# Seven-product up projection of a fused decoder trunk: three products chained in one PSUM bank, the seventh one pair later

## The chip, the cores and the metric

One core of a Trainium2 chip. The metric is the device time of one execution of the whole program in microseconds.

## The reference

Two decoder layers over 1024 tokens of width 1024, all in float32. Layer 0 mixes with a gated DeltaNet, layer 1 with gated linear attention; after each mixer stands a feed-forward block, the part that the change touches:

```python
def conv_glu_ffn(h, w_up, conv_w, w_down):          # h (1, 1024, 1024), w_up (1024, 5632), w_down (2816, 1024)
    u = causal_depthwise_conv(h @ w_up, conv_w)     # 3 taps over the tokens, one set per channel
    gate, val = jnp.split(u, 2, axis=-1)
    return (jax.nn.silu(gate) * val) @ w_down
...
x = x + rms_norm(conv_glu_ffn(rms_norm(x, ffn_pre_norm[layer]), ...), ffn_post_norm[layer])
```

## The kernel before

**Matmuls.** Every float32 operand is kept as a high and a low part (fp32r). A product is three matmuls with 512 columns: high by high, high by low, low by high (`product3`, lines 80 to 82). All engines run their own hand-ordered list; semaphores hold them together.

**Up stage.** The 5632 output channels are 44 tiles of 128: 22 gate tiles and 22 value tiles, in pairs p = 0 to 21. Tokens are split in a near and a far half of 512, input channels in halves k1 and k2. Pairs 0 to 3 are done plainly. From pair 4 (`PLAIN`) on, a pair's 2 x 2 block product (two weight tiles, two token halves) is done with seven quarter products instead of eight (Winograd's form of Strassen). The names A11, A12, A22 are weight blocks, S1 to S4 sums of weight blocks, made by POOL in `sums` (line 404); t1, t2, t4 are sums of token blocks. One quarter product is 4 x 3 matmuls. PE's order in a pair (`seven_products`) is A11, S2, S3, S1, A22, A12, S4. The first three go to three quarters of two PSUM tensors `part_ps`, S1 and A22 to the far and near half of `gate_ps`, A12 and S4 to the near and far half of `value_ps`. A half is one bank.

**What follows a product.** ScalarE copies A11's product to SBUF (`keep_first`, line 489). VectorE joins the rest in seven additions (`products`, helper `join`, line 707), among them those into gate far, gate near, value near and value far. Then for the gate and the value tile each: ScalarE writes the last tap times the PSUM tensor (`scaled_gate` line 467, `scaled_value` line 476), VectorE adds the two other taps (`conv`, lines 693 and 698), ScalarE takes silu of the gate (line 481), and VectorE multiplies both (`activated`, line 704). The hidden tile goes to DRAM by SyncE.

**Weights.** Raw tiles arrive in a ring of four (`raw`). ScalarE makes the high part (`high`, `high_operand`, line 439), POOL the low part (`low`, line 398), into a ring of ten half slots that runs ahead of PE; a slot is free when `s_prod` shows its product done.

**Down stage.** 22 steps d for the near tokens, then 22 for the far. A step reads one hidden tile back: SyncE loads it into one of three buffers `h_raw` (`load_hidden`, line 339; from d = 3 on it waits until `hidden_low(d - 3)` has freed the buffer), ScalarE makes the high part (`high_hidden`, line 497), VectorE the low part (`hidden_low`, line 712). A step is 4 x 2 x 3 matmuls into the four PSUM tensors `down_ps`; `part_ps`, both, come first, then `gate_ps`, then `value_ps`. In step 0 PE waits before the third for the last gate convolution and before the fourth for the last value convolution (`s_conv`).

**The last pair.** In pair 21 the lists of both stages interleave. ScalarE: ..., `scaled_gate`, `high_hidden(2)`, a down weight, `silu`, `high_hidden(3)`, `scaled_value`, a down weight, `high_hidden(4)`. VectorE: `hidden_low(0)` and `hidden_low(1)` stand ahead of the join that waits for A22:

```python
            if p == FT - 1:
                hidden_low(0)
                hidden_low(1)
            dve.wait_ge(s_prod, task(p, A22) + 1)
            join(gate_ps[:, near], u3, gate_ps[:, near])
            conv(2 * p, gate_ps, gate, near_value)
            dve.wait_ge(s_prod, task(p, S4) + 1)
            join(value_ps[:, far], with_p5, value_ps[:, far])
            conv(2 * p + 1, value_ps, hid[p % 2])
```

Of the kernel before, what the change touches and what calls it, by code (L numbers as in the profile page):

```python
# [6 lines left out]
P = 128  # L7
# [69 lines left out]
def product3(pe, out, w_hi, w_lo, x_hi, x_lo, first, last):  # L77


    pe.matmul(out, w_hi, x_hi, start=first, stop=False)  # L80
    pe.matmul(out, w_hi, x_lo, start=False, stop=False)  # L81
    return pe.matmul(out, w_lo, x_hi, start=False, stop=last)  # L82
# [105 lines left out]
def feed_forward(nc, stack, layer, consts, w_up, conv_w, w_down, hidden, x_in, x_out, post_gain, pre_gain, x_hi, x_lo,  # L188
# [38 lines left out]
    p1, u2, u3, with_p5 = (kept[:, n, :] for n in range(4))  # L227

    gate_ps = ahead.banks
    value_ps = ps(n_ + "value", [P, T])  # L230
    part_ps = [ps(f"{n_}part{i}", [P, T]) for i in range(2)]
    down_ps = [*part_ps, gate_ps, value_ps]
# [8 lines left out]
    s_p1 = sem("first_product_kept")  # L241
    s_comb = sem("products_joined")
# [20 lines left out]
    A11, S2, S3, S1, A22, A12, S4 = range(7)  # L263
    FIRST_DOWN = 2 * PLAIN + 7 * (FT - PLAIN)
# [4 lines left out]
    def task(pair, operand):  # L269
        return 2 * PLAIN + 7 * (pair - PLAIN) + operand  # L270
# [36 lines left out]
    def operand_source(k):  # L307

        pair, operand = PLAIN + (k - 2 * PLAIN) // 7, (k - 2 * PLAIN) % 7
# [4 lines left out]
    def joined(pair, n):  # L314
        return 7 * (pair - PLAIN) + n
# [4 lines left out]
    def _(sp):  # L320
# [10 lines left out]
        def load_hidden(d):  # L331
# [3 lines left out]
            if d >= HIDDEN_RAWS:  # L335
                sp.wait_ge(s_hlo, d - HIDDEN_RAWS + 1)
            elif PLAIN < FT:
                sp.wait_ge(s_lo, FIRST_DOWN)
# [56 lines left out]
    def _(pool):  # L395
# [10 lines left out]
        def operands(pair):  # L406
            gates, values = raw[2 * pair % FFN_RAWS], raw[(2 * pair + 1) % FFN_RAWS]
            made = 4 * (pair - PLAIN)
            for n in (2 * pair, 2 * pair + 1):
# [3 lines left out]
            low(task(pair, A11), values[:, near])  # L413
            low(task(pair, S2), sums[:, 1, :])
            combine(2, values[:, near], gates[:, near], ALU.subtract, 0)
            low(task(pair, S3), sums[:, 2, :])
            low(task(pair, S1), sums[:, 0, :])
            low(task(pair, A22), gates[:, far])
            combine(3, values[:, far], sums[:, 1, :], ALU.subtract, made + 2)
            low(task(pair, A12), values[:, far])  # L420
            low(task(pair, S4), sums[:, 3, :])
# [3 lines left out]
        for pair in range(PLAIN, FT):  # L425
            operands(pair)
        for d in range(STEPS):
# [7 lines left out]
    def _(act):  # L435
# [17 lines left out]

        def token_sum_high(n, out):
# [5 lines left out]
        def scaled_gate(p):  # L460
            if p < PLAIN:
                act.wait_ge(s_prod, 2 * p + 1)
            else:
                act.wait_ge(s_comb, joined(p, 5))
# [4 lines left out]
        def scaled_value(p):  # L469
            if p < PLAIN:  # L470
                act.wait_ge(s_prod, 2 * p + 2)
            else:
                act.wait_ge(s_comb, joined(p, 7))
            if p >= 2:
                act.wait_ge(s_store[p % 2], 16 * (p // 2))
            act.activation(hid[p % 2][:, :], value_ps[:, :], ACT.Copy, scale=taps[:, FT + p, 2:3]) \
# [63 lines left out]
        for p in range(PLAIN):  # L540
            if p < PLAIN - 1:
                high(2 * p + 2)
            else:
                for operand in (A11, S2, S3):
                    high_operand(PLAIN, operand)
# [11 lines left out]
            else:  # L557
# [3 lines left out]
                for operand in (S1, A22, A12):  # L561
                    high_operand(PLAIN, operand)
                scaled_gate(p)
                high_operand(PLAIN, S4)
            silu(p)
            scaled_value(p)
        for p in range(PLAIN, FT):
            if p < FT - 1:
                for operand in (A11, S2, S3):
# [60 lines left out]
    def _(dve):  # L630
# [155 lines left out]
        for p in range(PLAIN):  # L786
# [22 lines left out]
            conv(2 * p + 1, value_ps, hid[p % 2])  # L809
# [39 lines left out]
    def _(pe):  # L849
# [13 lines left out]
        def plain_pair(p):  # L863
            n = 2 * p
            if p < PLAIN - 1:
# [5 lines left out]
                up_half(n + 1, value_ps, near)  # L871
                up_half(n + 1, value_ps, far).then_inc(s_prod, 1)
            else:
# [3 lines left out]
                up_half(n + 1, value_ps, far).then_inc(s_b12, 1)  # L877
                up_half(n, gate_ps, near).then_inc(s_prod, 1)
                up_half(n + 1, value_ps, near).then_inc(s_prod, 1)

        def quarter_product(p, operand, out, high, low):
# [3 lines left out]
            for kt in range(KT // 2):  # L885
                f = slice(kt * P, (kt + 1) * P)
                last = product3(pe, out, part_of(w_hi, k)[:, f], part_of(w_lo, k)[:, f], high[:, kt, :],
                                low[:, kt, :], kt == 0, kt == KT // 2 - 1)
# [2396 lines left out]
```

## Time and profile before

| | us |
|---|---|
| median of 3 runs | 2660.61 |
| lowest, highest | 2660.61, 2661.56 |
| span of the profiled execution | 2660.1 |
| PE busy in it | 2594.3 (98%) |
| VectorE, POOL, ScalarE busy | 1637.7, 1180.7, 1116.7 |

The span runs from the first to the last instruction. The stages that the change touches are pairs 4 to 21 of the up stage and its seam to the down stage, once in each layer: about 877 to 1223 us and 2065 to 2416 us. Matmuls overlap: each is shown with some 0.39 us, and the time from one start to the next is what counts.

### The profile page before, as it was taken

What the parts mean: (1) busy time and instruction counts of PE and PEld (TensorE: products, weight loads), DVE (VectorE), ACT (ScalarE), POOL (GpSimd) and SP (SyncE); (2) the same over time, 40 slices, a digit from 0 to 9 for tenths busy, and PEclk for the clock granted to TensorE, in tenths of its full rate; (3) what the DMA queues carried; (4) which work ended last, traced back from release to release, by engine and by line L of the source; (5) the groups of instructions that cost most, each with busy time, mean ns of one, the idle gap of its engine ahead of it and who ended that gap; (6) DMA issues with size and microseconds to landing.
All of it is one profiled execution on the core that took longest, in us unless ns stands there. A gap on an engine that the chain in (4) does not pass through costs nothing. (4 is left out here: it accounts for less than half of the span.)

```text
span 2660.1 us, 34055 instructions
## 1 busy us (share of the span) xinstructions
PE 2594.3 (98%) x12821; PEld 2153.7 (81%) x12821; DVE 1637.7 (62%) x1743; ACT 1116.7 (42%) x1648; POOL 1180.7 (44%) x721
## 2 busy tenths in 40 slices
PE   7899999999999999999999999999999999999998
PEld 5788888888878888888888788888878888888887
DVE  5677666676177666665455657557557666665454
ACT  6445545545353443433344334434533434343242
POOL 2444333435313878774443111112413887874442
PEclk9999999999999999999999999999999999999999
DMA  3111011102342222224554111012521222224453
GB/s 121 30 43 47 32 41 46 47 32 73 95 146 78 87 72 96 72 95 159 180 173 137 58 32 48 24 55 70 166 98 64 87 84 84 80 99 155 171 189 115
DMA packets 84540, 238.06 MB, mean 89 GB/s; under 512 B 8928, under 2 KB 22816, under 8 KB 84416
## 3 DMA queue, kind: packets, MB, share of 16 engines
q1 hardware_dynamic: 84416, 236.39, 26.8%
q8 instruction: 80, 1.31, 0.2%
q14 instruction: 44, 0.36, 0.0%
HBM read 189.66 MB, written 46.69 MB: 89 GB/s over the span
## 5 line engine op out<-in xcount | busy, mean ns | idle before, releaser
L398 POOL TENSOR_TENSOR f_wlo<-f_raw,f_whi 128x512 fp32r<-128x512 f32 (+1 forms) x210 | 427.6, 2037 | 490.1 <-ACT f_whi L439 490.1
L712 DVE TENSOR_TENSOR f_hlo<-f_hraw,f_hhi 128x512 fp32r<-128x512 f32 x88 | 182.9, 2084 | 198.9 <-ACT f_hhi L497 198.9
L439 ACT ACTIVATE f_whi<-f_raw 128x512 fp32r<-128x512 f32 (+1 forms) x210 | 172.0, 834 | 269.2 <-PE f_value L82 252.2
L398 POOL TENSOR_TENSOR f_wlo<-f_sums,f_whi 128x512 fp32r<-128x512 f32 x144 | 188.5, 1319 | 39.8 <-ACT f_whi L439 39.8
L439 ACT ACTIVATE f_whi<-f_sums 128x512 fp32r<-128x512 f32 x144 | 90.4, 627 | 271.2 <-POOL f_sums L404 271.2
L80 PE MATMUL f_value<-x_hi,f_whi 128*128 128x512 f32 x416 | 162.7, 391 | 1.2 <-POOL f_wlo L398 1.2
L81 PE MATMUL f_value<-x_lo,f_whi 128*128 128x512 f32 x416 | 162.6, 391 | 0.0
L82 PE MATMUL f_value<-x_hi,f_wlo 128*128 128x512 f32 x416 | 162.5, 391 | 0.0
L80 PE MATMUL f_part<-f_whi,f_hhi 128*128 128x512 f32 x352 | 137.9, 392 | 0.0
L82 PE MATMUL f_part<-f_whi,f_hlo 128*128 128x512 f32 x352 | 137.5, 391 | 0.0
L81 PE MATMUL f_part<-f_wlo,f_hhi 128*128 128x512 f32 x352 | 137.1, 389 | 0.0
L1708 POOL TENSOR_TENSOR g_wlo_first<-g_raw_first,g_whi_first 128x1024 fp32r<-128x1024 f32 x15 | 36.7, 2449 | 201.8 <-ACT g_whi_first L1793 201.8
L707 DVE TENSOR_TENSOR f_kept<-f_part,f_kept 128x512 f32<-128x512 f32 x72 | 49.8, 692 | 108.3 <-ACT f_kept L489 103.2
L2723 POOL TENSOR_TENSOR l_wlo<-l_raw,l_whi 128x1024 fp32r<-128x1024 f32 x12 | 29.4, 2446 | 192.5 <-ACT l_whi L2752 192.5
L80 PE MATMUL banks<-x_hi,g_whi_first 128*128 128x512 f32 x256 | 110.1, 430 | 3.9 <-POOL g_wlo_first L1708 3.9
L82 PE MATMUL f_part<-x_hi,f_wlo 128*128 128x512 f32 x288 | 112.5, 390 | 0.0
L81 PE MATMUL f_part<-x_lo,f_whi 128*128 128x512 f32 x288 | 112.5, 390 | 0.0
L80 PE MATMUL f_part<-x_hi,f_whi 128*128 128x512 f32 x288 | 112.4, 390 | 0.0
L80 PE MATMUL banks<-x_hi,g_whi 128*128 128x512 f32 x256 | 109.2, 427 | 0.0
L481 ACT ACTIVATE f_gate<-f_gate 128x1024 f32<-128x1024 f32 x44 | 46.7, 1062 | 148.8 <-DVE f_gate L698 148.8
L82 PE MATMUL banks<-x_hi,g_wlo_first 128*128 128x512 f32 x256 | 101.0, 395 | 0.0
L81 PE MATMUL banks<-x_lo,g_whi_first 128*128 128x512 f32 x256 | 100.9, 394 | 0.0
(539 smaller groups left out, 7649.0 us busy)
## 6 DMA issues: line engine op xcount, KB each, us to landing
f_raw<-in_ffn_w_up SPq DMA_DIRECT2D x88, 512.0 KB, 3.6
f_raw<-in_ffn_w_down SPq DMA_DIRECT2D x88, 512.0 KB, 3.6
hidden<-f_hid SPq DMA_DIRECT2D x44, 512.0 KB, 2.7
f_hraw<-hidden SPq DMA_DIRECT2D x88, 256.0 KB, 4.0
g_raw_first<-in_gdn_w_in SPq DMA_DIRECT2D x16, 512.0 KB, 3.6
g_raw<-in_gdn_w_in SPq DMA_DIRECT2D x16, 512.0 KB, 4.2
f_xt<-x_mid SPq DMA_DIRECT2D x16, 512.0 KB, 4.8
l_raw_first<-in_gla_w_in SPq DMA_DIRECT2D x12, 512.0 KB, 3.5
```

Of the source, the lines that this page charges most:

```text
L80: pe.matmul(out, w_hi, x_hi, start=first, stop=False)
L81: pe.matmul(out, w_hi, x_lo, start=False, stop=False)
L82: return pe.matmul(out, w_lo, x_hi, start=False, stop=last)
L398: pool.tensor_tensor(part_of(w_lo, k), source, part_of(w_hi, k).bitcast(F32), ALU.subtract) \
L439: act.activation(part_of(w_hi, k), source, ACT.Copy).then_inc(s_hi, 1)
L481: act.activation(gate[:, :], gate[:, :], ACT.Silu).then_inc(s_silu, 1)
L707: dve.tensor_tensor(out, psum, kept_part, ALU.add).then_inc(s_comb, 1)
L712: dve.tensor_tensor(h_lo[d % FFN_SLOTS][:, :], h_raw[d % HIDDEN_RAWS][:, :], plain32(h_hi[d % FFN_SLOTS][:, :]), ALU.subtract).then_inc(s_ ...
L1708: pool.tensor_tensor(w_lo[s][:, :], raw[s][:, :], w_hi[s][:, :].bitcast(F32), ALU.subtract) \
L2723: pool.tensor_tensor(w_lo[s][:, :], raw[s][:, :], w_hi[s][:, :].bitcast(F32), ALU.subtract) \
```

## The change

- **PSUM.** `part_ps` becomes one tensor, of which one bank (`chain_ps`) is used in the up stage. The value tensor is doubled, `value_ps[p % 2]`. The four down tensors are now part, value 0, gate, value 1.
- **Products.** A11, S2 and S3 are accumulated in `chain_ps`, one on top of the other. ScalarE copies the partial sum out after each (`keep(p, 0)`, `(p, 1)`, `(p, 2)`: p1, u2, u3), and PE's next product in the bank waits for that copy. S1 goes to the far half of the value tensor. VectorE adds u3 to it into gate far. S4 is then accumulated on top of S1.
- **Order.** PE: A11 of pair p, S4 of pair p - 1, then S2, S1, S3, A22, A12 of pair p; S4 of the last pair stands alone. Operand order on ScalarE and POOL follows.
- **Joins.** VectorE does four instead of seven: gate far, gate near, value near, value far. The value tile's far join, last tap and convolution, silu and the final product move behind the start of the next pair.
- **Last pair.** `hidden_low(0)` and `(1)` now stand behind the gate convolution; ScalarE has `high_hidden(3)` ahead of `silu(21)` and `scaled_value(21)`. SyncE's first hidden loads wait for one operand fewer.

```diff
-    p1, u2, u3, with_p5 = (kept[:, n, :] for n in range(4))
+    p1, u2, u3 = (kept[:, n, :] for n in range(3))
 
     gate_ps = ahead.banks
-    value_ps = ps(n_ + "value", [P, T])
-    part_ps = [ps(f"{n_}part{i}", [P, T]) for i in range(2)]
-    down_ps = [*part_ps, gate_ps, value_ps]
+    value_ps = [ps(f"{n_}value{i}", [P, T]) for i in range(2)]
+    part_ps = ps(n_ + "part", [P, T])
+    chain_ps = part_ps[:, 0:HALF]
+    down_ps = [part_ps, value_ps[0], gate_ps, value_ps[1]]
...
-    A11, S2, S3, S1, A22, A12, S4 = range(7)
-    FIRST_DOWN = 2 * PLAIN + 7 * (FT - PLAIN)
+    A11, S4, S2, S1, S3, A22, A12 = range(7)
+    order = []
+    for pair in range(PLAIN, FT):
+        order.append((pair, A11))
+        if pair > PLAIN:
+            order.append((pair - 1, S4))
+        order += [(pair, operand) for operand in (S2, S1, S3, A22, A12)]
+    order.append((FT - 1, S4))
+    index = {which: 2 * PLAIN + n for n, which in enumerate(order)}
+    FIRST_DOWN = 2 * PLAIN + len(order)
...
-                sp.wait_ge(s_lo, FIRST_DOWN)
+                sp.wait_ge(s_lo, task(FT - 1, A12) + 1)
...
+            lows((pair, A11))
+            if pair > PLAIN:
+                lows((pair - 1, S4))
+            lows((pair, S2), (pair, S1))
...
+                act.wait_ge(s_c22, p - PLAIN + 1)
+                act.wait_ge(s_c21, p - PLAIN + 1)
...
-                act.wait_ge(s_comb, joined(p, 7))
+                act.wait_ge(s_c11, p - PLAIN + 1)
+                act.wait_ge(s_c12, p - PLAIN + 1)
...
-        def keep_first(pair):
-            act.wait_ge(s_prod, task(pair, A11) + 1)
-            if pair > PLAIN:
-                act.wait_ge(s_comb, joined(pair - 1, 6))
+        def keep(pair, n):
+
+            before = pair - PLAIN
+            operand, out, free = ((A11, p1, s_c11), (S2, u2, s_c12), (S3, u3, s_c21))[n]
+            act.wait_ge(s_prod, task(pair, operand) + 1)
+            if before:
+                act.wait_ge(free, before)
             else:
                 act.wait_ge(s_tlo, 8)
-            act.activation(p1, part_ps[0][:, near], ACT.Copy).then_inc(s_p1, 1)
+            act.activation(out, chain_ps, ACT.Copy).then_inc(s_kept, 1)
...
         for p in range(PLAIN, FT):
-            if p < FT - 1:
-                for operand in (A11, S2, S3):
-                    high_operand(p + 1, operand)
-                keep_first(p)
-                for operand in (S1, A22, A12, S4):
-                    high_operand(p + 1, operand)
-                scaled_gate(p)
-                silu(p)
-                scaled_value(p)
+            more = p < FT - 1
+            keep(p, 0)
+            if p > PLAIN:
+                silu(p - 1)
+            if more:
+                high_operands(p + 1, A11)
+            high_operands(p, S4)
+            if more:
+                high_operands(p + 1, S2)
             else:
                 high(2 * FT)
-                keep_first(p)
+            if p > PLAIN:
+                scaled_value(p - 1)
+            if more:
+                high_operands(p + 1, S1)
+            else:
                 high(2 * FT + 1)
                 high_hidden(0)
+            keep(p, 1)
+            if more:
+                high_operands(p + 1, S3, A22, A12)
+            else:
                 high(2 * FT + 2)
                 high_hidden(1)
-                scaled_gate(p)
+            keep(p, 2)
+            if not more:
                 high_hidden(2)
                 high(2 * FT + 3)
-                silu(p)
-                high_hidden(3)
-                scaled_value(p)
-                high(2 * FT + 4)
-                high_hidden(4)
+            scaled_gate(p)
+        high_hidden(3)
+        silu(FT - 1)
+        scaled_value(FT - 1)
+        high(2 * FT + 4)
+        high_hidden(4)
...
-        def join(out, kept_part, psum):
-            dve.tensor_tensor(out, psum, kept_part, ALU.add).then_inc(s_comb, 1)
...
-        def products(p):
-            def near_value():
+        def value_far(p):
+            dve.wait_ge(s_prod, task(p, S4) + 1)
+            dve.tensor_tensor(value_ps[p % 2][:, far], value_ps[p % 2][:, far], u2, ALU.add).then_inc(s_c12, 1)
+
+        def joins(p):
+            def value_near():
                 dve.wait_ge(s_prod, task(p, A12) + 1)
-                join(value_ps[:, near], p1, value_ps[:, near])
-
-            dve.wait_ge(s_prod, task(p, S2) + 1)
-            dve.wait_ge(s_p1, p - PLAIN + 1)
-            join(u2, p1, part_ps[0][:, far])
-            if p > PLAIN:
-                activated(p - 1)
-            dve.drain()
-            dve.wait_ge(s_prod, task(p, S3) + 1)
-            join(u3, u2, part_ps[1][:, near])
-            dve.drain()
-            dve.wait_ge(s_prod, task(p, S1) + 1)
-            join(with_p5, u2, gate_ps[:, far])
-            dve.drain()
-            join(gate_ps[:, far], u3, gate_ps[:, far])
-            if p == FT - 1:
-                hidden_low(0)
-                hidden_low(1)
+                dve.tensor_tensor(value_ps[p % 2][:, near], value_ps[p % 2][:, near], p1, ALU.add).then_inc(s_c11, 1)
+
+            dve.wait_ge(s_kept, 3 * (p - PLAIN) + 3)
+            dve.tensor_tensor(gate_ps[:, far], value_ps[p % 2][:, far], u3, ALU.add).then_inc(s_c22, 1)
             dve.wait_ge(s_prod, task(p, A22) + 1)
-            join(gate_ps[:, near], u3, gate_ps[:, near])
-            conv(2 * p, gate_ps, gate, near_value)
-            dve.wait_ge(s_prod, task(p, S4) + 1)
-            join(value_ps[:, far], with_p5, value_ps[:, far])
-            conv(2 * p + 1, value_ps, hid[p % 2])
+            dve.tensor_tensor(gate_ps[:, near], gate_ps[:, near], u3, ALU.add).then_inc(s_c21, 1)
+            conv(2 * p, gate_ps, gate, value_near)
...
-        activated(PLAIN - 1)
         for p in range(PLAIN, FT):
-            products(p)
+            if p > PLAIN:
+                value_far(p - 1)
+                conv(2 * p - 1, value_ps[(p - 1) % 2], hid[(p - 1) % 2])
+            activated(p - 1)
+            joins(p)
+        hidden_low(0)
+        hidden_low(1)
+        value_far(FT - 1)
+        conv(2 * FT - 1, value_ps[(FT - 1) % 2], hid[(FT - 1) % 2])
         activated(FT - 1)
...
+        def last_of_pair(p):
+
+            pe.wait_ge(s_c22, p - PLAIN + 1)
+            quarter_product(p, S4, value_ps[p % 2][:, far], x_hi[:, k2, far], x_lo[:, k2, far], False, True)
+
         def seven_products(p):
-            later = p > PLAIN
-            if later:
-                pe.wait_ge(s_p1, p - PLAIN)
-            quarter_product(p, A11, part_ps[0][:, near], x_hi[:, k1, near], x_lo[:, k1, near])
-            if later:
-                pe.wait_ge(s_comb, joined(p - 1, 1))
+            n = p - PLAIN
+            value = value_ps[p % 2]
+            if n:
+                pe.wait_ge(s_kept, 3 * n)
+            quarter_product(p, A11, chain_ps, x_hi[:, k1, near], x_lo[:, k1, near], True, False)
+            if n:
+                last_of_pair(p - 1)
             else:
                 pe.wait_ge(s_tlo, 8)
-            quarter_product(p, S2, part_ps[0][:, far], t2_hi, t2_lo)
-            if later:
-                pe.wait_ge(s_comb, joined(p - 1, 2))
-            quarter_product(p, S3, part_ps[1][:, near], x_hi[:, k1, far], x_lo[:, k1, far])
+            pe.wait_ge(s_kept, 3 * n + 1)
+            quarter_product(p, S2, chain_ps, t2_hi, t2_lo, False, False)
+            pe.wait_ge(s_conv, 2 * p - 2)
+            quarter_product(p, S1, value[:, far], t1_hi, t1_lo, True, False)
+            pe.wait_ge(s_kept, 3 * n + 2)
+            quarter_product(p, S3, chain_ps, x_hi[:, k1, far], x_lo[:, k1, far], False, True)
             pe.wait_ge(s_conv, 2 * p - 1)
-            quarter_product(p, S1, gate_ps[:, far], t1_hi, t1_lo)
-            quarter_product(p, A22, gate_ps[:, near], t4_hi, t4_lo)
-            pe.wait_ge(s_conv, 2 * p)
-            quarter_product(p, A12, value_ps[:, near], x_hi[:, k2, near], x_lo[:, k2, near])
-            quarter_product(p, S4, value_ps[:, far], x_hi[:, k2, far], x_lo[:, k2, far])
+            quarter_product(p, A22, gate_ps[:, near], t4_hi, t4_lo, True, True)
+            quarter_product(p, A12, value[:, near], x_hi[:, k2, near], x_lo[:, k2, near], True, True)
...
+        last_of_pair(FT - 1)
...
                     if j == 0:
-                        pe.wait_ge(s_p1, FT - PLAIN)
-                        pe.wait_ge(s_comb, joined(FT - 1, 1))
-                    elif j == 1:
-                        pe.wait_ge(s_comb, joined(FT - 1, 2))
+                        pe.wait_ge(s_kept, 3 * (FT - PLAIN))
```

## Rows read from the trace of the kernel before

**Rows 1.** Page, part 1: busy time, share and instructions of each engine.

```profile
PE 2594.3 (98%) x12821; PEld 2153.7 (81%) x12821; DVE 1637.7 (62%) x1743; ACT 1116.7 (42%) x1648; POOL 1180.7 (44%) x721
```

**Rows 2.** Waits of PE, whole span: us in total, times, longest.

```profile
PE f_value L80 <- DVE f_hid L698: 1.6, 2, 0.8
...
PE f_value L80 <- POOL f_wlo L398: 1.2, 2, 0.6
```

**Rows 3.** Busy PE by stretch: PE busy (instructions), PEclk, DMA, GB/s.

```profile
2066.00:2400.00 334.00, 334.00 (x1465) 1.00 0.25 85
```

**Rows 4.** Timeline, start, us: a pair's first two products; the keep.

```profile
2391.20 0.39 PE L80 MATMUL f_part<-x_hi,f_whi 128*128 128x512 f32 x1
...
2393.92 0.39 PE L80 MATMUL f_part<-f_t2hi,f_whi 128*128 128x512 f32 x1
...
2394.12 0.60 ACT L489 ACTIVATE f_kept<-f_part 128x512 f32<-128x512 f32 x1
```

**Rows 5.** By source line (min/median/max ns); a copy waiting in the timeline.

```profile
L489 ACT ACTIVATE f_kept<-f_part x36: 578/581/598, 881.4 to 2394.1; 128x512 f32<-128x512 f32 x36
...
L707 DVE TENSOR_TENSOR f_kept<-f_part,f_kept x35: 691/692/694, 2074.4 to 2396.8; 128x512 f32<-128x512 f32 x35
...
L404 POOL TENSOR_TENSOR f_sums<-f_raw,f_raw x36: 1302/1311/2297, 855.6 to 2377.1; 128x512 f32<-128x512 f32 x36
...
2378.49 0.63 ACT L439 ACTIVATE f_whi<-f_sums 128x512 fp32r<-128x512 f32 x1 [3.43 <-POOL f_sums L404]
```

**Rows 6.** Timelines, last pair of layer 1: DVE, ACT, SyncE's queue, PE.

```profile
2403.67 1.28 DVE L712 TENSOR_TENSOR f_hlo<-f_hraw,f_hhi 128x512 fp32r<-128x512 f32 x2
2405.00 0.70 DVE L707 TENSOR_TENSOR banks<-banks,f_kept 128x512 f32<-128x512 f32 x1
2406.88 1.28 DVE L693 SCALAR_TENSOR_TENSOR f_gate<-banks,f_taps,f_gate 128x1023 f32<-128x1023 f32 x1 [1.19 <-ACT f_gate L467]
...
2408.86 1.28 DVE L698 SCALAR_TENSOR_TENSOR f_gate<-banks,f_taps,f_gate 128x1022 f32<-128x1022 f32 x1
...
2405.73 1.12 ACT L467 ACTIVATE f_gate<-banks,f_taps 128x1024 f32<-128x1024 f32 x1 [4.53 <-DVE banks L707]
...
2410.18 1.06 ACT L481 ACTIVATE f_gate<-f_gate 128x1024 f32<-128x1024 f32 x1 [1.87 <-DVE f_gate L698]
2411.15 0.61 ACT L497 ACTIVATE f_hhi<-f_hraw 128x512 fp32r<-128x512 f32 x1
2411.66 1.10 ACT L476 ACTIVATE f_hid<-f_value,f_taps 128x1024 f32<-128x1024 f32 x1
...
2404.43 0.33 SPq L339 DMA_DIRECT2D f_hraw<-hidden  x1
...
2410.39 0.39 PE L80 MATMUL f_part<-f_whi,f_hhi 128*128 128x512 f32 x1
...
2415.49 0.50 PE L80 MATMUL f_value<-f_whi,f_hhi 128*128 128x512 f32 x1 [0.82 <-DVE f_hid L698]
```

**Rows 7.** Hidden loads: ACT's wait for one; issue to landing, both layers.

```profile
2421.80 0.63 ACT L497 ACTIVATE f_hhi<-f_hraw 128x512 fp32r<-128x512 f32 x1 [3.49 <-DMA f_hraw<-hidden]
...
DMA to landing us min/median/max: 3.5/4.0/4.7
...
DMA to landing us min/median/max: 3.2/4.0/4.9
```

**Rows 8.** PE after a long stop; two stretches with PEclk as above.

```profile
68.11 0.50 PE L80 MATMUL banks<-x_hi,g_whi_first 128*128 128x512 f32 x1 [3.88 <-POOL g_wlo_first L1708]
...
68.91 0.59 PE L80 MATMUL banks<-x_hi,g_whi_first 128*128 128x512 f32 x1
...
72.55 0.39 PE L80 MATMUL banks<-x_hi,g_whi_first 128*128 128x512 f32 x1
...
68.94:72.35 3.41, 3.41 (x10) 0.50 0.57 154
...
1477.00:1480.50 3.50, 1.01 (x7) 1.00 0.01 2
```

More of the change, by code:

```diff
@@ L74, in semaphores, with product3 @@
     return sem
[L77 to L82, printed above, removed]
+def product3(pe, out, w_hi, w_lo, x_hi, x_lo, first, last, read_between=False):
+    pe.matmul(out, w_hi, x_hi, start=first, stop=False, skip_group_check=read_between)
+    pe.matmul(out, w_hi, x_lo, start=False, stop=False, skip_group_check=read_between)
+    return pe.matmul(out, w_lo, x_hi, start=False, stop=last, skip_group_check=read_between)
 def product2(pe, out, w_both, x_hi, x_lo, first, last):
@@ L240, in feed_forward @@
     s_t, s_thi, s_tlo = sem("token_sum_made"), sem("token_sum_high"), sem("token_sum_low")
-    s_p1 = sem("first_product_kept")
-    s_comb = sem("products_joined")
+    s_kept = sem("partial_product_kept")
+    s_c11, s_c12, s_c21, s_c22 = (sem(f"joined_{x}") for x in ("value_near", "value_far", "gate_near", "gate_far"))
     s_taps = sem("taps_loaded")
@@ L269, in task @@
     def task(pair, operand):
-        return 2 * PLAIN + 7 * (pair - PLAIN) + operand
+        return index[pair, operand]
     def place(k):
@@ L307, in operand_source @@
     def operand_source(k):
-        pair, operand = PLAIN + (k - 2 * PLAIN) // 7, (k - 2 * PLAIN) % 7
+        pair, operand = order[k - 2 * PLAIN]
         gates, values = raw[2 * pair % FFN_RAWS], raw[(2 * pair + 1) % FFN_RAWS]
@@ L312, in operand_source @@
                 S3: sums[:, 2, :], S4: sums[:, 3, :]}[operand]
-    def joined(pair, n):
-        return 7 * (pair - PLAIN) + n
     block = ctx.enter_context(nc.Block())
@@ L408, in operands, with lows @@
             made = 4 * (pair - PLAIN)
+            def lows(*some):
+                for which in some:
+                    low(task(*which), operand_source(task(*which)))
             for n in (2 * pair, 2 * pair + 1):
@@ L412, in operands @@
             combine(1, sums[:, 0, :], values[:, near], ALU.subtract, made + 1)
-            low(task(pair, A11), values[:, near])
-            low(task(pair, S2), sums[:, 1, :])
+            lows((pair, A11))
+            if pair > PLAIN:
+                lows((pair - 1, S4))
+            lows((pair, S2), (pair, S1))
             combine(2, values[:, near], gates[:, near], ALU.subtract, 0)
-            low(task(pair, S3), sums[:, 2, :])
-            low(task(pair, S1), sums[:, 0, :])
-            low(task(pair, A22), gates[:, far])
+            lows((pair, S3), (pair, A22))
             combine(3, values[:, far], sums[:, 1, :], ALU.subtract, made + 2)
-            low(task(pair, A12), values[:, far])
-            low(task(pair, S4), sums[:, 3, :])
+            lows((pair, A12))
         for n in range(1, 2 * PLAIN):
@@ L426, in _ @@
             operands(pair)
+        low(task(FT - 1, S4), sums[:, 3, :])
         for d in range(STEPS):
@@ L452, in high_operand, with high_operands @@
             copy(k, operand_source(k))
+        def high_operands(pair, *some):
+            for operand in some:
+                high_operand(pair, operand)
         def token_sum_high(n, out):
@@ L543, in _ @@
             else:
-                for operand in (A11, S2, S3):
-                    high_operand(PLAIN, operand)
+                high_operands(PLAIN, A11, S2, S1)
             if p == 0:
@@ L560, in _ @@
                     token_sum_high(6 + c, x_hi[:, 2 * c:2 * c + 2, far])
-                for operand in (S1, A22, A12):
-                    high_operand(PLAIN, operand)
+                high_operands(PLAIN, S3, A22, A12)
                 scaled_gate(p)
-                high_operand(PLAIN, S4)
             silu(p)
@@ L808, in _ @@
                 third_difference(0)
-            conv(2 * p + 1, value_ps, hid[p % 2])
+            conv(2 * p + 1, value_ps[p % 2], hid[p % 2])
             if p < PLAIN - 1:
                 activated(p)
-        activated(PLAIN - 1)
         for p in range(PLAIN, FT):
-            products(p)
+            if p > PLAIN:
[7 more added lines that the diff above has]
+        conv(2 * FT - 1, value_ps[(FT - 1) % 2], hid[(FT - 1) % 2])
         activated(FT - 1)
@@ L870, in plain_pair @@
                 ready(n + 1)
-                up_half(n + 1, value_ps, near)
-                up_half(n + 1, value_ps, far).then_inc(s_prod, 1)
+                up_half(n + 1, value, near)
+                up_half(n + 1, value, far).then_inc(s_prod, 1)
             else:
@@ L876, in plain_pair, with quarter_product @@
                 ready(n + 1)
-                up_half(n + 1, value_ps, far).then_inc(s_b12, 1)
+                up_half(n + 1, value, far).then_inc(s_b12, 1)
                 up_half(n, gate_ps, near).then_inc(s_prod, 1)
-                up_half(n + 1, value_ps, near).then_inc(s_prod, 1)
-        def quarter_product(p, operand, out, high, low):
+                up_half(n + 1, value, near).then_inc(s_prod, 1)
+        def quarter_product(p, operand, out, high, low, fresh, final):
             k = task(p, operand)
@@ L887, in quarter_product @@
                 last = product3(pe, out, part_of(w_hi, k)[:, f], part_of(w_lo, k)[:, f], high[:, kt, :],
-                                low[:, kt, :], kt == 0, kt == KT // 2 - 1)
+                                low[:, kt, :], fresh and kt == 0, final and kt == KT // 2 - 1, operand in (A11, S2, S3, S1, S4))
             last.then_inc(s_prod, 1)
+        def last_of_pair(p):
+            pe.wait_ge(s_c22, p - PLAIN + 1)
+            quarter_product(p, S4, value_ps[p % 2][:, far], x_hi[:, k2, far], x_lo[:, k2, far], False, True)
@@ L891, in seven_products @@
         def seven_products(p):
-            later = p > PLAIN
-            if later:
-                pe.wait_ge(s_p1, p - PLAIN)
-            quarter_product(p, A11, part_ps[0][:, near], x_hi[:, k1, near], x_lo[:, k1, near])
-            if later:
-                pe.wait_ge(s_comb, joined(p - 1, 1))
+            n = p - PLAIN
+            value = value_ps[p % 2]
+            if n:
+                pe.wait_ge(s_kept, 3 * n)
+            quarter_product(p, A11, chain_ps, x_hi[:, k1, near], x_lo[:, k1, near], True, False)
```

4 lines of the change are left out of this document (1 added, 3 removed).

## Prediction, made before the change was run

> **What bounds the kernel now.** I read the engine shares first: the matmul engine is busy for 2594.3 of 2660.1 us [rows 1]. Then the waits of that engine alone, over the whole span. Of the two feed-forward stages they hold only two lines [rows 2]: 1.6 us in two waits of 0.8 us for line 698 (the second step of a convolution), and 1.2 us in two waits of 0.6 us for the first value weights. The table of stretches says the same of the pairs of the second layer: 334.00 us busy in 334.00, granted clock 1.00 [rows 3]. So in the up stage every microsecond that PE loses is lost at the end, and nothing that merely makes VectorE or ScalarE faster is worth anything. The most that the change can win back there is those two waits of 0.8 us, plus the restart.
>
> **The pace.** A quarter product is 12 matmuls; the first of A11 starts at 2391.20 and the first of S2 at 2393.92 [rows 4], so 2.72 us a product and 0.227 us a matmul. Each pair has seven products, 19.04 us. Before and after the change this count is the same: 18 pairs in each of 2 layers, 3024 matmuls. What can move is waiting only.
>
> **The steady state.** VectorE loses three joins of 512 columns a pair, 0.69 us each; ScalarE gains two keeps of 0.58 us [rows 5]. Neither bounds. The new waits of PE, with t = 0 at the start of A11 of pair p (order A11, S4 of the pair before, S2, S1, S3, A22, A12):
> - S2 waits for the keep of A11. A11 ends at 2.72, ScalarE starts the keep 0.2 later (2394.12, where S2's first matmul starts at 2393.92 [rows 4]), the keep ends near 3.5; S2 is due at 5.44. Slack 1.9 us, behind S4.
> - S3 waits for the keep of S2. S2 ends at 8.16; the keep is 8.4 to 9.0, if ScalarE is free. Queued ahead of it are silu (1.06), four operand copies (0.63 each [rows 5]; back to back one every 0.5) and the value's last tap (1.10; both [rows 6]), which itself waits for S4's join (5.7 to 6.4). That queue ends near 8.0. S3 is due at 10.88: slack 1.9 us.
> - The copy of S3 for the next pair waits for a POOL sum, 3.43 us in the trace before [rows 5]. In the new order it stands behind the keep of S2, not ahead, and keep three is not due until the next A11 at 19.04 (the join behind it until 21.8). POOL has four sums and seven differences as wide, 1.3 us each in the median, some 14.3 us of 19.04; the longest is 2.3 us [rows 5], and even three such in a pair leave over 1.5 us.
> - S4 waits for the far gate join: made by 15.1, due at 21.8. A22 and S1 wait for convolutions that ended at 2.7 or a pair earlier, due at 13.6 and 8.16. SyncE stores a hidden tile about 5 us later than before, but the loads queued behind it wait until 14.6 anyway for POOL, and are for a pair two ahead.
> Cost of the steady state: 0, hidden behind S4 and S1. If ScalarE were over 1.9 us late in each pair it would cost the excess 36 times.
>
> **The first of the seven-product pairs.** There is no earlier S4 to put behind A11, so S2 follows it at once. PE then stands from 2393.92 (as it would be) until the keep's end, 2394.12 + 0.60, plus 0.05: 0.85 us [rows 4]. A first matmul after a wait takes 0.50 instead of 0.39 [rows 6], so 0.1 more: 0.95 us a layer. ScalarE is free by then: its last task before, a tap of 1.1 us, waits for the product that ends where A11 begins, 2.72 us earlier. Bounds 0.8 to 1.5.
>
> **The last pair, where the sum is made.** Here I followed every wait that is moved. Before, `hidden_low(0)` and `(1)` stood on VectorE ahead of the A22 join: 2403.67, two in 1.28 us; SyncE issued the fourth hidden load (it reuses the first buffer) at 2404.43; it had long landed when ScalarE came to it. PE began the down projection at 2410.39 and had to stop only at its fourth PSUM tensor, until line 698 ended: 2415.49 [rows 6].
> After, these two stand behind the whole gate convolution, and ScalarE has `high_hidden(3)` ahead of both the last silu and the last tap. On the clock of the trace before, with S4 ending where it did:
> 1. A22's end is seen at 2405.00. A down weight copy, 1024 columns like silu (behind which the next start came 0.97 later, 2410.18 to 2411.15), now goes ahead of the tap: tap 2406.0 to 2407.1, 0.25 later than 2405.73.
> 2. The gate convolution took from 2406.88 to 2408.86 + 1.28 = 2410.14, 3.26 us; now 2407.1 to 2410.4.
> 3. `hidden_low(0)`: 0.65, until 2411.0. PE needs it for its first down step, due at 2410.39: a stop of 0.6 to 0.7.
> 4. SyncE issues the load at 2411.1. Landing takes 4.0 us in the median, 3.2 to 4.9 at the ends, in both layers [rows 7]. Landed: 2415.1.
> 5. ScalarE: high part (next start 0.51 later, 2411.15 to 2411.66), silu (0.97), tap 1.10 long: 2415.15 + 0.51 + 0.97 + 1.10 = 2417.75. Behind the waiting high part stand silu, tap, the fifth weight copy. VectorE's value join is over at 2412.4 and does not count.
> 6. Value convolution and the start of PE's fourth tensor: 2.73 us behind the tap, as before (2411.66 + 1.10 = 2412.76, PE 2415.49). So 2420.5.
> Before 2415.49, after 2420.5 to 2420.6: 5.1 us a layer. The old loss before that tensor (18 matmuls from 2410.39 end at 2414.5, so 0.98 us) is already inside the 2415.49, and the stop of step 3 is hidden in the 5.1. PE's three other tensors take 4.1 us, from 2411.0 to 2415.1, so one unbroken stop of about 5.4 us follows. The third down step is due at 2427.4 (6 matmuls, then 24), 6.9 us on; two VectorE operations stand before its `hidden_low(2)`: no further stop. Bounds: landing 3.2 or 4.9 gives 4.3 to 6.0.
> The Trainium skill ("DMA: Bandwidth & Descriptors", section Anatomy of one DMA) gives about 2.0 us of fixed cost; with 256 KB at the 436 GB/s of that section's fit I estimate 2.6 us to landing, and the whole change would be 2.8 us cheaper by it. These stretches of the trace have no hidden load under 3.2 us, so the sum stays with the trace.
>
> **The clock.** With PE stopped for 3.88 us until 68.11, the granted clock was at half (1.2 GHz) from 68.94 to 72.35. Nine matmuls then went from 68.91 to 72.55, 3.64 us instead of 9 x 0.227 = 2.04: 1.6 us lost. Elsewhere PE was busy for only 1.01 of 3.50 us and the clock stayed at 1.00 [rows 8]. So a stop of 5.4 us very likely brings a fall, of which part may lie in the stop itself: I take 1.2 us a layer, bounds 0 and 3.1 (two such falls). The Trainium skill ("TensorE: Matmul & The Clock Gate", Part 1) says "the default state is throttled, and activity releases the throttle"; the trace agrees.
>
> **The sum.** (0.95 + 5.1 + 1.2) x 2 = 14.5 us. The profiled execution's span is 2660.1, the median of the runs 2660.61, so 0.5 us lie around the span. 2660.6 + 14.5 = 2675.1 us, +0.54%.
>
> **Rivals.**
> - *Same or slightly faster.* The second value tensor and fewer joins free the end of the pair, and the fourth hidden load does not sit in the chain (that is, the last silu and tap run as early as before). Then the waits of 0.98 + 0.1 us vanish at most: 2 x (0.95 - 1.1) = -0.3 us. The pace is the second source: over the long stretch it is 334.00/1465 = 0.228 us a matmul [rows 3] against 0.227. If the joins' PSUM traffic caused the difference, 3024 x 0.0013 = 3.9 us were to be had: 2656 to 2661. It decides for "not slower" only if steps 3 and 4 are wrong. Against it: the code makes ScalarE wait for the fourth landing in order, and the slower pace comes and goes across products of every kind. A clear gain would need over 5.3 us, more than all waits plus the pace can give at once. The engine's full busy row speaks against it.
> - *ScalarE late in every pair.* If its queue reached the keep of S2 over 1.9 us late, S3 would stop 36 times; 1 us each makes 2711 us. For it: ScalarE's largest waits are for POOL, whose operations stretch to 2.3 us. Against it: those waits are behind that keep now.
> - *The stop without the clock.* 12.1 us, 2672.7; with short landings too 10.5 us.
>
> Measuring this kernel can tell about 0.2%, 5.3 us, from no change.
>
> **Chances.** Forecast, with or without the fall of the clock: 0.83. Late in every pair: 0.05. Not slower: 0.12, of it 0.02 by more than 5.3 us. So slower 0.88, same 0.10, faster 0.02. Range: low end short landings and no fall, with the first pair's bound, 2 x (0.8 + 4.2) = 10, less 1 for a chain that runs a little tighter: 2669.5. High end: 2 x (1.0 + 6.0 + 3.1) = 20.2 us: 2681. That holds the forecast's cases; the others fill the rest.
>
> **What would show it.** Right: PE's waits after the change hold one of about 0.8 us for a keep in each layer, one of 0.5 to 0.7 for the first `hidden_low`, and one of 5 to 5.5 for line 698's successor; the fourth high part on ScalarE waits for a DMA; the granted clock shows 0.50 near each up-to-down seam. Wrong: the long wait is absent, or PE waits for keeps in every pair.

## The result and the profile after

| | before | after |
|---|---|---|
| median, us | 2661.09 (4 runs) | 2676.21 (4 runs) |
| lowest, highest, us | 2660.61, 2661.6 | 2674.36, 2677.31 |
| span of the profiled execution, us | 2660.1 | 2675.4 |

The ratio is 1.0055, 95% interval 1.0043 to 1.0067: 15 us slower. The forecast was 2675.1 us.

The engine shares come first (page, part 1, of the kernel after). They answer to [rows 1]: VectorE has 79 us less to do than before, ScalarE 39 us more, PE the same 12821 matmuls. The kernel is slower all the same.

```profile
PE 2599.1 (97%) x12821; PEld 2156.3 (81%) x12821; DVE 1558.4 (58%) x1635; ACT 1156.0 (43%) x1720; POOL 1156.6 (43%) x721
```

PE's own waits in the feed-forward stages, kernel after (waited for: us in total, times, longest). These answer to [rows 2], where line 698 stood for 1.6 us; that instruction is line 725 now.

```profile
PE f_value L80 <- DVE f_hid L725: 8.3, 2, 4.2
...
PE f_part L80 <- issue: 2.6, 4, 0.7
```

The four waits of at most 0.7 us are two in each layer: the chain's second product in pair 4 and the first down step. The two of 4.2 us stand before the fourth down tensor. The stretch of the pairs is almost as full as in [rows 3]; the same view of the kernel after (PE busy, instructions, granted clock):

```profile
2066.00:2400.00 334.00, 333.27 (x1461) 1.00 0.26 85
```

The 0.73 us that it lacks are one wait, at the chain's second product in pair 4, so none of the other pairs in it waits. PE's timeline of the kernel after:

```profile
2076.33 0.47 PE L80 MATMUL f_part<-f_t2hi,f_whi 128*128 128x512 f32 x1 [0.73 <-issue]
```

The last pair of layer 1, kernel after: timelines of VectorE, ScalarE, SyncE's queue and PE. They answer to [rows 6].

```profile
2413.44 0.70 DVE L751 TENSOR_TENSOR banks<-banks,f_kept 128x512 f32<-128x512 f32 x1 [1.39 <-PE banks L82]
...
2417.58 1.28 DVE L725 SCALAR_TENSOR_TENSOR f_gate<-banks,f_taps,f_gate 128x1022 f32<-128x1022 f32 x1
2418.78 1.28 DVE L736 TENSOR_TENSOR f_hlo<-f_hraw,f_hhi 128x512 fp32r<-128x512 f32 x2
2419.98 0.69 DVE L741 TENSOR_TENSOR f_value<-f_value,f_kept 128x512 f32<-128x512 f32 x1
...
2414.47 1.10 ACT L483 ACTIVATE f_gate<-banks,f_taps 128x1024 f32<-128x1024 f32 x1
2422.75 0.63 ACT L517 ACTIVATE f_hhi<-f_hraw 128x512 fp32r<-128x512 f32 x1 [7.18 <-DMA f_hraw<-hidden]
2423.28 1.04 ACT L498 ACTIVATE f_gate<-f_gate 128x1024 f32<-128x1024 f32 x1
2424.23 1.10 ACT L493 ACTIVATE f_hid<-f_value,f_taps 128x1024 f32<-128x1024 f32 x1
...
2419.54 0.33 SPq L345 DMA_DIRECT2D f_hraw<-hidden  x1
...
2419.57 0.47 PE L80 MATMUL f_part<-f_whi,f_hhi 128*128 128x512 f32 x1 [0.56 <-issue]
...
2423.54 0.39 PE L82 MATMUL banks<-f_whi,f_hlo 128*128 128x512 f32 x1
...
2428.06 0.80 PE L80 MATMUL f_value<-f_whi,f_hhi 128*128 128x512 f32 x1 [4.12 <-DVE f_hid L725]
```

Read in the order of cause. The gate convolution ends (2417.58 + 1.28); only then comes `hidden_low(0)`; at 2419.54 SyncE issues the fourth hidden load and at 2419.57 PE starts the first down step. ScalarE idles 7.18 us until the landing (the load is not even issued for the first 4.0 of them), though the gate is ready for silu from 2418.86 and the value for its tap from 2420.67, where its far join ended. Then come high part, silu and tap, and PE goes on at 2428.06.

The granted clock behind the two stops, kernel after (busy PE by stretch, PEclk is the third figure); compare [rows 8].

```profile
1228.55:1232.47 3.92, 3.92 (x10) 0.56 0.36 127
2427.14:2433.96 6.82, 5.90 (x14) 0.50 0.50 145
```

**Where the 15.3 us of the two spans went.** Both kernels issue the same number of matmuls in sizes that match one for one, so the start times can be subtracted matmul by matmul. The difference grows at four places in each layer (the last three make up the seam, where the up stage ends and the down stage begins):

| place | layer 0, us | layer 1, us |
|---|---|---|
| pair 4, second product of the chain, with its restart | 1.01 | 1.02 |
| the 17 pairs behind it | 0.00 | 0.00 |
| first down step | 0.72 | 0.72 |
| fourth down tensor | 3.46 | 3.39 |
| slow matmuls behind it (clock at 1.2 GHz) | 1.62 | 2.75 |
| sum | 6.81 | 7.89 |

The remaining 0.6 us arise outside these stages, where the granted clock also falls at other moments than in the kernel before.

### The profile page after: what moved, and what is told of

It reads as the page before. It is cut to its first block and busy times, and to the rows that moved or that the text cites. A ratio compares the mean times of both kernels' runs of the same rounds, so it can differ in the third digit from the quotient of the medians.

```text
span 2675.4 us, 33983 instructions
## 1 busy us (share of the span) xinstructions
PE 2599.1 (97%) x12821; PEld 2156.3 (81%) x12821; DVE 1558.4 (58%) x1635; ACT 1156.0 (43%) x1720; POOL 1156.6 (43%) x721
## 5 line engine op out<-in xcount | busy, mean ns | idle before, releaser
L404 POOL TENSOR_TENSOR f_wlo<-f_raw,f_whi 128x512 fp32r<-128x512 f32 (+1 forms) x210 | 396.4, 1889 | 521.3 <-ACT f_whi L450 521.3
L80 PE MATMUL f_value<-f_whi,f_hhi 128*128 128x512 f32 x352 | 139.1, 395 | 8.3 <-DVE f_hid L725 8.3
L82 PE MATMUL f_value<-f_whi,f_hlo 128*128 128x512 f32 x352 | 138.3, 393 | 0.0
L81 PE MATMUL f_value<-f_wlo,f_hhi 128*128 128x512 f32 x352 | 137.8, 392 | 0.0
L509 ACT ACTIVATE f_kept<-f_part 128x512 f32<-128x512 f32 x108 | 64.6, 598 | 163.5 <-PE f_part L82 163.5
L81 PE MATMUL banks<-x_lo,g_whi 128*128 128x512 f32 x256 | 100.4, 392 | 0.0
```

The source lines that it names most:

```text
L80: pe.matmul(out, w_hi, x_hi, start=first, stop=False, skip_group_check=read_between)
L81: pe.matmul(out, w_hi, x_lo, start=False, stop=False, skip_group_check=read_between)
L82: return pe.matmul(out, w_lo, x_hi, start=False, stop=last, skip_group_check=read_between)
L404: pool.tensor_tensor(part_of(w_lo, k), source, part_of(w_hi, k).bitcast(F32), ALU.subtract) \
L509: act.activation(out, chain_ps, ACT.Copy).then_inc(s_kept, 1)
```

## Experiments

"By matmul" means: taken from the start times as in the table above, against the profiled kernel before. Each ratio is against runs of the kernel before made in the same session, with medians of 2661.15 us (E1, E2, B1, E3) and 2661.60 us (the others). The theory is that the order of VectorE and ScalarE at the seam and the bare chain in pair 4 cost everything. The rival is that the new product chain itself costs it.

**E1: the two `hidden_low` back ahead of the A22 join.**

```diff
             dve.tensor_tensor(gate_ps[:, far], value_ps[p % 2][:, far], u3, ALU.add).then_inc(s_c22, 1)
+            if p == FT - 1:
+                hidden_low(0)
+                hidden_low(1)
             dve.wait_ge(s_prod, task(p, A22) + 1)
...
-        hidden_low(0)
-        hidden_low(1)
         value_far(FT - 1)
```

> Theory (order at the seam): with hidden_low(0) and (1) back ahead of the A22 join, the fourth hidden load is issued some 6 us earlier and has landed when ScalarE comes to it. PE's stop before the first down step (0.8 us) vanishes and the one before the fourth down tensor falls from 4.2 to about 1 us in each layer; no fall of the granted clock there. Left over: the first pair's 0.9 us a layer. 2660.6 + 1.9 + 0.5 = about 2663 us. Rival (the new product chain costs the time: three keeps, S4 on top of S1, value far joined late): the stop before the fourth tensor stays near 4 us, 2674 us or more.

Measured: 2664.45 us, ratio 1.0013 (1.0004 to 1.0023), against 1.0055 with the change as it is. PE's waits in this run:

```profile
PE f_part L80 <- issue: 1.5, 2, 0.7
...
PE f_value L80 <- DVE f_hid L725: 1.1, 2, 0.6
```

Two of the four small waits are gone, and the two large ones fell from 4.2 to 0.6 us, under the 0.8 us of the kernel before. No fall of the clock stands at a seam. By matmul the seam costs nothing (0.00 us at the first down step, -0.25 us at the fourth tensor, in each layer); the 1.0 us of pair 4 is left. ScalarE's order is still the changed one here, so that order alone costs nothing while the load is issued early. The rival's 2674 us is out. The median is 1.4 us above the forecast. By matmul this trace is 3.2 us behind the kernel before: 1.5 at these places, 1.2 already at pair 4 of layer 0, 0.5 between the layers' stages.

**E2: ScalarE's fourth high part behind the last silu and tap, all else as changed.**

```diff
-        high_hidden(3)
         silu(FT - 1)
         scaled_value(FT - 1)
+        high_hidden(3)
         high(2 * FT + 4)
```

> Theory: with ScalarE's fourth high part behind the last silu and tap, the landing leaves the chain, though the load is still issued late. The stop before the first down step stays (0.8 us a layer), the two hidden_low delay the value's far join by about 0.8 us, so the fourth down tensor starts 0.8 us a layer later than in the kernel before, against 3.4 + 0.8 more in the changed one. No clock fall. 2660.6 + 1.9 + 1.6 to 2.5 = 2664 to 2665 us. Rival (VectorE's order alone makes the stop, the landing is innocent): the stop before the fourth tensor stays over 3 us, 2672 us or more.

Measured: 2665.36 us, ratio 1.0015 (1.0006 to 1.0025). The load is still issued late (2413.97, beside PE's first down step at 2414.00), but silu and tap no longer stand behind it. ScalarE's timeline in layer 1, then PE's waits in this run:

```profile
2413.33 1.06 ACT L498 ACTIVATE f_gate<-f_gate 128x1024 f32<-128x1024 f32 x1 [3.33 <-DVE f_gate L725]
2415.19 1.12 ACT L493 ACTIVATE f_hid<-f_value,f_taps 128x1024 f32<-128x1024 f32 x1 [0.80 <-DVE f_value L741]
2416.78 0.63 ACT L517 ACTIVATE f_hhi<-f_hraw 128x512 fp32r<-128x512 f32 x1 [0.47 <-DMA f_hraw<-hidden]
```

```profile
PE f_part L80 <- issue: 2.6, 4, 0.7
...
PE f_value L80 <- DVE f_hid L725: 1.4, 2, 0.7
```

All four small waits are there, as in the change, and the large ones are not. By matmul: 0.72 us at the first down step, -0.05 us at the fourth tensor. The fourth tensor was forecast 0.8 us later than in the kernel before in each layer; it was 0.7 later. VectorE's order alone makes the 0.7 us. It takes both, the late load (absent in E1) and the landing ahead of silu and tap in ScalarE's queue (absent here), to make the other 3.4.

The trace has one fall of the clock that the change has not, at 1480.52 us, for 3.41 us. It is in neither feed-forward stage; it is taken up under E135.

**B1: the kernel before with the seam's order alone.**

```diff
-            if p == FT - 1:
-                hidden_low(0)
-                hidden_low(1)
...
             conv(2 * p, gate_ps, gate, near_value)
+            if p == FT - 1:
+                hidden_low(0)
+                hidden_low(1)
...
-                scaled_gate(p)
                 high_hidden(2)
                 high(2 * FT + 3)
-                silu(p)
+                scaled_gate(p)
                 high_hidden(3)
+                silu(p)
                 scaled_value(p)
```

> The kernel before with nothing but the seam's order of the changed one (hidden_low(0) and (1) behind the gate convolution; the fourth high part ahead of silu and tap). Theory: all of the seam's loss is there without any of the new products: a stop of 0.8 us before the first down step and of about 4 us before the fourth tensor in each layer, 2 x 4.3 = 8.6 us, plus clock falls of 1.6 to 3 us a layer: 2660.6 + 8.6 + 3 to 5 = 2672 to 2675 us. Rival (the loss needs the new product chain): 2661 to 2663 us.

Measured: 2676.12 us, ratio 1.005 (1.0034 to 1.0067). Almost the whole loss is there without a single new product, keep or PSUM bank. PE's waits in this run:

```profile
PE f_value L80 <- DVE f_hid L698: 8.3, 2, 4.2
...
PE f_part L80 <- issue: 1.1, 2, 0.6
```

By matmul: 0.72 us at the first step and 3.41 and 3.44 us at the fourth tensor, the same as in the change, and 2.81 and 1.62 us of slow matmuls behind it. This time the long fall is in layer 0 and the short one in layer 1. The seams sum to 12.7 us; another 2.2 us of this trace arise outside them. That the median equals the change's 2676.21 us, which has 2.0 us of pair 4 besides, is therefore in part luck; it lies 1.1 us above the top of the forecast.

**E3: pair 4 in another order.** PE, ScalarE and POOL take A11, S1, S2, A22, S3, A12 in pair 4, so that a product lies between the products of the chain there too.

```diff
-        order += [(pair, operand) for operand in (S2, S1, S3, A22, A12)]
+        order += [(pair, operand) for operand in ((S2, S1, S3, A22, A12) if pair > PLAIN else (S1, S2, A22, S3, A12))]
...
```

> The changed kernel with another order in pair 4 alone: A11, S1, S2, A22, S3, A12, so that a product lies between the chain's products there too. Theory: PE's two waits of 0.7 to 0.8 us at the second product of pair 4 vanish, 1.8 us less than the changed kernel: about 2674.4 us, seam as before the edit. Rival (these waits are hidden by something later or come back at another place of the pair): 2676 us, as the changed kernel, with a wait elsewhere in pair 4.

Measured: 2672.86 us, ratio 1.0045 (1.0029 to 1.0062). PE has no wait at all between 860 and 900 us in this trace, and by matmul the term of pair 4 is 0.00 in both layers. 1.8 us less than the change was expected and 3.4 us less measured, with intervals that overlap the change's; what follows is read from the trace. By matmul the feed-forward stages give 2.7 us (14.70 to 11.97), 2.0 of them in pair 4. The other 0.7 are the landing and the clock: in layer 1 the fourth hidden load landed sooner. ScalarE's and PE's timelines there:

```profile
2419.10 0.63 ACT L517 ACTIVATE f_hhi<-f_hraw 128x512 fp32r<-128x512 f32 x1 [6.78 <-DMA f_hraw<-hidden]
...
2424.40 0.50 PE L80 MATMUL f_value<-f_whi,f_hhi 128*128 128x512 f32 x1 [3.75 <-DVE f_hid L725]
```

The load was issued at 2416.29, so ScalarE had it after 2.81 us (3.21 in the change), and the stop by matmul is 2.99 instead of 3.39 us: 0.4 for 0.4.

**E6: the stop filled with work done twice.** Down step 0's matmuls into the first three tensors are issued once more and overwrite themselves, 36 more matmuls in all. No other engine's order or waits are changed.

```diff
             step_ready(d)
+            if d == 0:
+                pe.wait_ge(s_kept, 3 * (FT - PLAIN))
+                for j in range(NT // 2 - 1):
+                    if j:
+                        pe.wait_ge(s_conv, 2 * FT - 3 + j)
+                    for half in range(2):
+                        down(d, j, half, True, True)
             for j in range(NT // 2):
...
```

> The changed kernel, its stop before the fourth down tensor filled with work that is done twice: the matmuls of down step 0 into the first three tensors (18, 4.1 us a layer) are issued once more and overwrite themselves. The dependences are the same; only PE is not idle. Theory (part of the loss is the granted clock falling after the stop): no fall to half at either seam; the fourth tensor starts at the same moment as before the edit or up to 0.1 us later; 4.3 us less than the changed kernel (1.6 and 2.7 us in the two layers): about 2672 us, in spite of 36 more matmuls. Rival (the fall costs nothing that the stop did not already cost): 2676 us; or, if PE had other work to do in the stop, more.

Measured: 2673.56 us, ratio 1.0049 (1.0033 to 1.0064), 2.7 us under the change by the medians; with these intervals the runs alone do not settle it. The trace does. The seams of this run, some 24 us each (busy PE by stretch, PEclk is the third figure):

```profile
1216.00:1240.00 24.00, 23.38 (x103) 1.00 0.57 196
2415.50:2440.00 24.50, 22.71 (x100) 1.00 0.53 180
```

ScalarE's and PE's timelines of this run in layer 1:

```profile
2421.17 0.63 ACT L517 ACTIVATE f_hhi<-f_hraw 128x512 fp32r<-128x512 f32 x1 [8.32 <-DMA f_hraw<-hidden]
...
2426.48 0.50 PE L80 MATMUL f_value<-f_whi,f_hhi 128*128 128x512 f32 x1 [1.23 <-DVE f_hid L725]
```

The clock stays at 1.00, and the term of the slow matmuls is 0.02 and 0.00 us instead of 1.62 and 2.75. So the two falls cost 4.35 us, and the stops caused them. The fourth tensor starts 3.39 us late in layer 0 (3.46 without the filling), but 4.54 instead of 3.39 in layer 1: that load was issued at 2416.82 and ScalarE had it only 4.35 us later. This ate 1.1 us of the 4.3 that were forecast; the fall described under E135 is in this trace too and in the change's is not.

**E13 and E135: both repairs; and the first two down steps mixed.** E13 is E1 and E3 together. E135 also does the first three tensors of steps 0 and 1 before the fourth of both:

```diff
...
+        for d in range(2):
+            step_ready(d)
+            for j in range(NT // 2 - 1):
+                if d == 0 and j:
+                    pe.wait_ge(s_conv, 2 * FT - 3 + j)
+                for half in range(2):
+                    down(d, j, half, d == 0, False)
+        pe.wait_ge(s_conv, 2 * FT)
+        for d in range(2):
+            for half in range(2):
+                last = down(d, NT // 2 - 1, half, d == 0, False)
+            last.then_inc(s_prod, 1)
+        for d in range(2, FT):
...
```

> The changed kernel with both repairs: hidden_low(0) and (1) ahead of the A22 join, and pair 4 in the order A11, S1, S2, A22, S3, A12. Theory: all that the change lost is accounted for by these two places: the time is that of the kernel before within 0.5 us, 2660.6 to 2661.5 us, with PE's wait of 0.8 us a layer before the fourth down tensor left. Rival (the new chain also costs or gains in the pairs themselves, through PSUM or ScalarE): off by 2 us or more.

> As the run with both repairs, and PE does the first three down tensors of steps 0 and 1 before the fourth tensor of both, so that 36 matmuls (8.2 us) instead of 18 lie over the last value convolution. Theory: the last wait of 0.8 us a layer goes too, with its restart 2.1 us together: 2658.5 to 2659.5 us. Rival (the wait comes back in steps 1 to 4, as their buffers are freed later): 2660.6 us or more.

E13 measured 2661.57 us, ratio 0.9998 (0.9989 to 1.0007): the change without its two losses is the kernel before. By matmul it is 0.25 us a layer ahead, all at the fourth tensor. E135 measured 2659.87 us, ratio 0.9995 (0.9986 to 1.0004). Its trace has no wait left on the last convolution, and by matmul it is 1.12 us a layer ahead. Those 2.2 us are seen in the trace; the runs cannot tell them from nothing, and the median is 0.4 us above the forecast.

The trace shows what stands against them. Where layer 1 begins, PE stops for 2.5 us in every one of the ten traces. In the kernel before, the change, E1, B1, E3 and E13 the clock stayed at 1.00 there. In E2, E6, E135 and B5 it fell to half for 3.41 us, and the matmuls behind it started 1.6 us later. PE's timeline in the kernel before and in E2, and a stretch of E2:

```profile
1479.90 0.40 PE L87 MATMUL l_pm<-x_hi,l_small_w 128*32 128x512 f32 x1 [2.49 <-PEq L71]
...
1480.06 0.40 PE L87 MATMUL l_pm<-x_hi,l_small_w 128*32 128x512 f32 x1 [2.52 <-PEq L71]
...
1480.52:1483.94 3.42, 3.42 (x10) 0.50 0.73 191
```

**B5: the kernel before with the first two steps mixed**, same edit.

> The kernel before, with only the first two down steps mixed in the same way. Theory: the same 2.1 us less than before, 2658.5 us, without any of the change: then the doubled value tensor and the chain bring nothing of their own. Rival: the mixing needs the new layout; 2660.6 us.

Measured: 2660.43 us, ratio 0.9996 (0.9987 to 1.0005), and by matmul the same 1.12 us a layer. The median lies 1.9 us above the theory's 2658.5 us and next to the rival's 2660.6, so the runs do not decide; the matmul starts do, against the rival. Once the steps are mixed, the chain and the doubled value tensor bring nothing of their own.

## Why the prediction was right, and where it was not

- *PE bounds, and the pairs cost nothing.* Right: the start times of the two kernels stay 0.00 us apart through the 17 pairs, in both layers. Fewer joins and another use of PSUM did not change the pace, so the rival's 3.9 us do not exist. The slack of 1.9 us was right too: from the end of the keep of S2 to the start of S3 the trace has 1.92 to 2.00 us in pairs 4 to 20 of both layers. In the last pair the keep ran from 2405.88 to 2406.46 and S3 started at 2407.80, 1.3 us to spare: it stood behind a weight copy and a high part, which only the last pair has.
- *The first of the seven-product pairs.* 0.95 us a layer forecast, 1.01 and 1.02 measured; E3 removes it.
- *The last pair, steps 1 to 3.* Right: the stop before the first down step was said to be 0.6 to 0.7 us; it is 0.72, restart included. On the clock of the trace before (8.44 us less, by the last matmuls of the up stage) the load was issued at 2411.10; 2411.1 had been said.
- *Step 4, the landing.* Mis-sized. 4.0 us was taken, the median of [rows 7]. From issue to ScalarE's start it took 3.21 us in layer 1 and 3.27 in layer 0. Of the eight such loads in the change, B1, E3 and E6, six took 3.18 to 3.27 us, one 2.81 (E3) and one 4.35 (E6), and the stop followed the landing one for one. The median taken was over several loads; the fourth load itself had landed after 3.2 and 3.5 us in the kernel before, which would have been the nearer value. The term of the seam was therefore 4.2 and 4.1 us instead of 5.1, and the longest wait 4.2 us instead of the 5 to 5.5 that had been named as its sign. The prediction's estimate of 2.6 us was reached by none, though E3 came within 0.2 us. It was taken from the Trainium skill ("DMA: Bandwidth & Descriptors", section Anatomy of one DMA), whose fit is stated there for DMAs that GpSimd issues; these loads are issued by SyncE.
- *Steps 5 and 6.* Right: from the landing to PE's start 5.31 us (2422.75 to 2428.06); 0.51 + 0.97 + 1.10 + 2.73 = 5.31 had been worked out (the sum printed as 2417.75 is 2417.73).
- *The clock.* Right in kind, mis-sized: 1.2 us a layer taken, 1.62 and 2.75 measured. In layer 1 the half clock (1.2 GHz) lasted 6.8 us, 0.9 of it in the stop; a stretch that long was in the bounds, not in the value taken. E6 shows that the stop is its cause.
- *The sum.* 14.5 forecast, 15.3 in the spans. The seam was 1.9 us smaller than said, the clock 2.0 us larger, pair 4 0.1 larger, and 0.6 came from stages that were not touched. The total is closer than its terms because two errors of almost 2 us each cancelled; that is luck. The high end of the range also took 1.0 us for pair 4 where its own bound was 1.5; nothing hung on it.
- *The rivals.* "Same or slightly faster" named its own condition, that the fourth load does not sit in the chain. E2 makes this true by moving one line, and the median is 10.9 us lower than the change's, but still 4.2 us above the kernel before: step 3's stop is left. E1, without steps 3 and 4, shows that the rival's price was too low as well: 0.76 us a layer by matmul instead of -0.15, because PE's wait before the fourth tensor shrank only from 0.8 to 0.6 us. "ScalarE late in every pair" did not occur.

What stays open is why the same load takes 2.8 us once and 4.35 us another time. What went on beside it does not tell: in the change, B1, E3 and E6 no DMA moved a byte in the 4 us before it was issued, and the same two loads followed 0.37 and 0.90 us behind it. No run varied this. Open too is why the same 2.5 us stop at the start of layer 1 let the clock fall in four traces and not in six.

## What to carry to other kernels

In a hand-ordered list, an instruction that waits for a DMA also holds everything written behind it, and the DMA may itself wait for a step of another engine that the same edit moved. Follow each moved step through its whole circle (VectorE frees the buffer, SyncE issues, ScalarE waits, VectorE waits for ScalarE, PE waits for VectorE) at the first and the last trip of the loop, where the work that hides it inside the loop is missing. When the engine that bounds is never idle inside the loop, only those seams can gain. Inside the loop an edit can only lose, and here the slack of 1.9 us kept it from that.

## What the runs showed of the hardware

Every stop of PE of 3.75 to 4.2 us at a seam brought a fall of the granted clock to 0.50 (the change, B1, E3: six stops, six falls). In three the clock fell before PE was back at work; these stretches at half lasted 6.8 us and cost 2.5 to 2.8 us. In the other three it fell 0.3 to 1.5 us after PE was back, for 3.4 us, and cost 1.6 us. Each of the three kernels had one of each kind. Waits of 0.6 to 1.2 us brought none at these seams (E1, E2, E6). A stop of 2.5 us elsewhere brought one in four traces out of ten, for 3.4 us and at 1.6 us, so one trace with or without a fall does not say what a stop of that size costs. The fourth hidden load took 2.81 to 4.35 us from SyncE's issue to ScalarE's start (eight times in the change, B1, E3 and E6), with no byte moved by a DMA in the 4 us before its issue. Three products added up in one bank, read by ScalarE between them, ran at the same pace as separate banks: 0.00 us over 17 pairs.
